# A deeper ring for expert weights, with gate and up weights signalled apart, in a mixture-of-experts inference step

## What is computed

```python
    eidx = gsel[:, None] * EXPERTS_PER_GROUP + top_i      # 2 of 32 experts for each token
    for e in range(N_EXPERTS):
        he = jax.nn.silu(hf @ w_gate[e]) * (hf @ w_up[e])
        out = out + combine[:, e:e + 1] * (he @ w_down[e])
    ...
    shf, scf = jnp.split((jax.nn.silu(c) @ w_ada_f + b_ada_f)[:, None, :], 2, axis=-1)
    return modulate(rms_norm(x, g_final), shf, scf)
```

## Time and profile before

| what | value |
|---|---|
| time, median of 3 runs | 886.25 us (883.65 to 887.63) |
| time of the profiled execution | 883.69 us |
| its span, first to last instruction | 881.9 us |
| mean granted TensorE clock | 0.952 of full |
| TensorE busy with matmuls | 794.0 us (90%) |
| VectorE busy | 526.8 us (60%) |
| ScalarE busy | 226.2 us (26%) |
| bytes moved by DMA | 203.57 MB, 231 GB/s over the span |

### The profile page before, as it was taken

How to read it: one execution, slowest core, us unless ns; L and a number is a source line. 1 busy time by engine, 2 the same in 40 slices (tenths; PEclk the granted TensorE clock), 3 DMA queues, 4 the chain that set the end, 5 groups by cost and what they waited for, 6 DMA issues and landing times. The chain is left out here.

```text
span 881.9 us, 12815 instructions
## 1 busy us (share of the span) xinstructions
PE 794.0 (90%) x5326; PEld 622.1 (71%) x5330; DVE 526.8 (60%) x779; ACT 226.2 (26%) x322; POOL 64.5 (7%) x113
## 2 busy tenths in 40 slices
PE   3799999989999999999999998179999997988876
PEld 1499997546889999999999687156666564544532
DVE  1768999999758799956554774813233223132146
ACT  4353233010423233267123232012111101010003
POOL 1100000000000000000000000012222222111110
PEclk9899999999999999999999999569999999897899
DMA  9935433797753123232444515969999999899925
GB/s 339 338 90 152 150 131 101 265 327 247 244 179 84 56 72 96 72 94 75 131 123 147 197 54 220 399 211 399 360 373 415 417 394 411 332 420 408 379 95 236
DMA packets 96302, 203.57 MB, mean 231 GB/s; under 512 B 9725, under 2 KB 68453, under 8 KB 79856
## 3 DMA queue, kind: packets, MB, share of 16 engines
q1 hardware_dynamic: 81760, 160.28, 50.4%
q10 hardware_dynamic: 8960, 33.36, 9.5%
q0 software_dynamic: 5520, 9.06, 2.8%
HBM read 198.84 MB, written 14.84 MB: 242 GB/s over the span
## 5 line engine op out<-in xcount | busy, mean ns | idle before, releaser
L1515 DVE SCALAR_TENSOR_TENSOR arena<-arena,VT 128x574 f32<-128x574 f32 x240 | 177.1, 808 | 0.1
L964 PE MATMUL PS<-arena 128*64 128x256 f32 (+1 forms) x1024 | 147.3, 409 | 24.8 <-issue 20.5
L964 PEld LDWEIGHTS PS<-arena 128*64 128x64 f32 (+1 forms) x1024 | 105.4, 156 | 58.9 <-issue 34.2
L680 PE MATMUL PS<-gH,wHA 128*128 128x272 f32 x608 | 126.8, 290 | 0.8 <-ACT arena L1148 0.8
L680 PE MATMUL PS<-gH,wLA 128*128 128x272 f32 x608 | 126.5, 289 | 0.0
L680 PE MATMUL PS<-gL,wHA 128*128 128x272 f32 x608 | 126.3, 289 | 0.0
L680 PEld LDWEIGHTS PS<-gH,wHA 128*128 128x128 f32 x608 | 94.7, 188 | 7.3 <-ACT arena L1148 4.4
L680 PEld LDWEIGHTS PS<-gH,wLA 128*128 128x128 f32 x608 | 95.8, 188 | 0.0
L680 PEld LDWEIGHTS PS<-gL,wHA 128*128 128x128 f32 x608 | 95.2, 189 | 0.0
L1823 DVE TENSOR_TENSOR arena<-PS,arena 128x256 f32<-128x256 f32 x19 | 8.1, 424 | 134.2 <-ACT arena L1266 134.2
L984 PE MATMUL PS<-arena 128*64 128x512 f32 (+1 forms) x256 | 69.1, 597 | 1.4 <-DVE arena L1827 1.4
(11 more groups left out here) (313 smaller groups left out, 1137.6 us busy)
## 6 DMA issues: line engine op xcount, KB each, us to landing
arena<-w_gate SPq DMA_DIRECT2D x31, 1024.0 KB, 10.9
arena<-w_up SPq DMA_DIRECT2D x31, 1024.0 KB, 17.8
arena<-w_down ACTq DMA_DIRECT2D x27, 1024.0 KB, 10.7
arena<-w_ada SPq DMA_DIRECT2D x24, 1024.0 KB, 6.7
arena<-w_in SPq DMA_DIRECT2D x40, 512.0 KB, 4.2
arena<-w_ada_f SPq DMA_DIRECT2D x8, 1024.0 KB, 5.0
arena<-x_prompt SPq DMA_DIRECT2D x8, 512.0 KB, 7.4
arena<-w_in SPq DMA_DIRECT2D x4, 1024.0 KB, 6.3
```

The costliest lines, as they stand in the source:

```text
L680: last = pe.matmul(PS[:, bank + h, 0:H], w[:, k, :], part[:, k, h * H:(h + 1) * H], start=(k == 0 and n == 0), stop=(k == KT - 1 and n == 2))
L964: last = pe.matmul(PS[h * rows:(h + 1) * rows, 2, n * DE:(n + 1) * DE], hG[:, b, k * SLOTS + h * rows:k * SLOTS + (h + 1) * rows], buf[r][ ...
L1515: dve.scalar_tensor_tensor(out=total, in0=src, scalar=tap, in1=total, op0=ALU.mult, op1=ALU.add).then_inc(conv_step, 1)
```

## The change

- The ring has five places for all loads: load n goes to place `n % 5`, the load before it in the place is n - 5.
- Gate and up loads have semaphores of their own (`gate_full`, `up_full`; the latter are taken over from earlier stages). `gate_up` waits for the tile's gate loads, multiplies, raises `gate_done`, then waits for its up loads, multiplies, raises `gu_done`.
- SyncE loads a gate array when `gate_done`, and an up array when `gu_done`, has reached the last use of the place. The expert's number is read ahead of both waits.
- The down loads of loads 30 and 31 are issued in tile 18 (elsewhere still in the tile after the last use of the place), behind a new wait of ScalarE for the up half of load 31.
- The final vectors are loaded after the down loads of 30 and 31 have landed and the up product of tile 18 is done (place 4 now holds load 29 until then).
- Four semaphores that only count begun steps become one.

```diff
-        gu_full = [sem(f"gu_full{r}") for r in range(5)]
+        gate_full = [sem(f"gate_full{r}") for r in range(5)]
+
+        up_full = ada1_in[TT:KT] + [ws_in, cache_in]
+        gate_done = sem("gate_done")
...
         def place_of(n):
-            return n if n < NSTATIC else (n - 1) % 4
+            return n % NSTATIC
 
         def before_it(n):
-            return n - 5 if n < NSTATIC + 4 else n - 4
+            return n - NSTATIC
 
         def uses(n):
-            return 1 if n < NSTATIC else (n - 1) // 4 + 1
+            return n // NSTATIC + 1
...
             for n in range(NSTATIC, LOADS):
+                e = owner_of(unit_of(n))
+                sp.wait_ge(gate_done, last_use[before_it(n)])
+                load_gate(place_of(n), e)
                 sp.wait_ge(gu_done, last_use[before_it(n)])
-                load_owned(unit_of(n), place_of(n))
-
+                load_up(place_of(n), e)
+
+            for n in in_tile[ALWAYS]:
+                sp.wait_ge(wd_full[place_of(n)], 16 * uses(n))
+            sp.wait_ge(gu_done, last_use[LOADS - 3])
             sp.dma_start(gfb, a["g_final"].rearrange("(o n) -> o n", o=1).to_broadcast([P, D])).then_inc(fin_in, 16)
...
-                slots = weights(i, t, gu_full, 32)
                 pe.wait_ge(hg_ready, cnt(i, t, 2))
-                rows = SLOTS // len(slots)
-                for n, buf in enumerate((WG, WU)):
+                for n, (buf, full_of, done) in enumerate(((WG, gate_full, gate_done), (WU, up_full, gu_done))):
+                    slots = weights(i, t, full_of, 16, 16 * n)
+                    rows = SLOTS // len(slots)
                     for k in range(KT):
                         for h, r in enumerate(slots):
                             last = pe.matmul(PS[h * rows:(h + 1) * rows, 2, n * DE:(n + 1) * DE],
...
-                last.then_inc(gu_done, 1)
+                    last.then_inc(done, 1)
...
                     for n in range(NSTATIC, LOADS):
-                        if last_use[before_it(n)] == t - 1:
+                        if t == (ALWAYS - 1 if n in in_tile[ALWAYS] else last_use[before_it(n)] + 1):
+                            if n == in_tile[ALWAYS][0]:
+                                act.wait_ge(up_full[place_of(LOADS - 1)], 16 * uses(LOADS - 1) + 16)
                             load_d(unit_of(n), place_of(n))
```

More of the change, by code:

```diff
@@ L262, in build @@
         mod_stored = [sem("mod_stored0"), sem("mod_stored1")]
-        loads_begun, turns_begun, gathers_begun, scatters_begun = (sem(n) for n in ("loads_begun", "turns_begun", "gathers_begun", "scatters_begun"))
+        begun = sem("begun")
         ada1_in = [sem(f"ada1_in{k}") for k in range(KT)]
@@ L937, in turn_rows @@
                 pe.wait_ge(gathered[b], cnt(i, t, 8, 8 * (1 - b)))
-                pe.sem_inc(turns_begun)
+                pe.sem_inc(begun)
                 if t >= 2:
                     pe.wait_ge(hg_ready, cnt(i, t, 2, -2))
-                    pe.sem_inc(turns_begun)
+                    pe.sem_inc(begun)
                 for k in range(KT):
@@ L944, in turn_rows, with weights @@
                 last.then_inc(t_ps, 1)
-            def weights(i, t, full_of, per):
+            def weights(i, t, full_of, per, earlier=0):
                 if t <= ALWAYS:
                     for n in in_tile[t]:
-                        pe.wait_ge(full_of[place_of(n)], per * uses(n))
+                        pe.wait_ge(full_of[place_of(n)], per * uses(n) + earlier)
                     return [place_of(n) for n in in_tile[t]]
                 for r, more in later(t):
-                    pe.wait_ge(full_of[r], cnt(i, t, per // 2, per // 2 * more))
+                    pe.wait_ge(full_of[r], cnt(i, t, per // 2, per // 2 * more + earlier))
                 return [r for r, more in later(t)]
             def gate_up(i, t, b):
-                slots = weights(i, t, gu_full, 32)
                 pe.wait_ge(hg_ready, cnt(i, t, 2))
-                rows = SLOTS // len(slots)
-                for n, buf in enumerate((WG, WU)):
+                for n, (buf, full_of, done) in enumerate(((WG, gate_full, gate_done), (WU, up_full, gu_done))):
+                    slots = weights(i, t, full_of, 16, 16 * n)
+                    rows = SLOTS // len(slots)
                     for k in range(KT):
```

29 lines of the change are left out of this document (16 added, 13 removed).

## The result

The change makes the kernel faster, by less than half of what was forecast. The median goes from 886.53 us (20 runs) to 880.35 us (20 runs, 876.52 to 884.76); the ratio is 0.9933 with a 95% interval of 0.992 to 0.9947, thus about 6 us, or 0.7%. The forecast was 873.4 with a range of 868 to 881.5.

A forecast was written before the change was run, and what follows sets the result against it. The kernel was taken to wait for weights, DMA being by turns full and held by the four-place ring. -8.5 -0.5 -4.5 +0.3 +0.3 = -12.9 us took the median from 886.25 to 873.4 us, range 868 to 881.5.

The forecast's parts named there:

- E: End of kernel: final vectors issued after the last down loads land make VectorE wait; cost 0.3 us, upper end 3.
- A: Weight ring: five places close the DMA holes in the experts' stage; gain 8.5 us, bounds 4.2 and 12.
- B: Last tiles: deferring down loads 30 and 31 gains 0.5 us; undeferred with five places they would take 5 us.
- U: Last tile: the moment up load 31 lands, 828.74 us in the profile before; expected at about 820 after the change.
- D: Last tile: the last down product may wait for its deferred loads; cost 0.3 us, range 0 to 6.5.
- so DMA needn't stand: Step of A: three experts' gate and up loads under way (15 us) outlast a tile's product, at most 10.08 us.
- one hole whose cause the issue times prove: DMA hole from 750 to 770 us, laid to SyncE issuing 24's gate load only at 761.59; worth 4.2 us.
- C: Last tile: the gate half runs while the up load is in flight; gain 4.5 us, range 2.6 to 6.5.
- rivals 1 and 4: First: ring gains little, 881, chance 0.09; fourth: gate half doesn't run ahead, 878, chance 0.10 shared with a middling A.
- little comes of the ring: DMA holes move instead of closing, as SyncE stands at two waits per load; 5 us less, 881, chance 0.09.
- The third one: End of kernel: deferred down loads and final vectors land late, costing 9.9 us; 3 us slower, 889, chance 0.06.
- DMA share of 0.97 or more until the last up load: Sign that the forecast is right: this share in every 20 us from 630 us on in the experts' stage.

The follow-up runs named there:

- e1: Kernel after, with ScalarE issuing the final vectors right behind down load 31, without waiting for its landing: 875.59 us, ratio 0.9883.
- e2: Kernel before (four places, its due times), with only gate and up loads split onto semaphores of their own: 881.87 us, ratio 0.994.
- e3: Kernel after, but gate and up not apart: products wait for both halves, places refill after the up product: 884.01 us, ratio 0.9973.
- e13: Kernel before, with each expert's rows laced over a half and the two halves levelled: 878.64 us, ratio 0.9914.
- e6: Kernel after without deferring down loads 30 and 31; final vectors wait only for tile 18's product: 880.14 us, ratio 0.9939.
- e14: e6 (five places, split, nothing deferred) with rows laced and halves levelled: 871.80 us, ratio 0.9842.
- e11: Kernel after, with each expert's rows laced over a half and the two halves levelled: 874.24 us, ratio 0.9862.
- e8: Kernel after, with each unit's rows turned round by twice the unit's number: 880.44 us, ratio 0.9933.
- e16: Kernel after, with down loads and final vectors in SyncE's queue in order of use, rows laced and halves levelled: 868.78 us, ratio 0.9809.
- e5: Kernel after without the expert stage's gathers and scatters, one even 0.46 MB ScalarE store a tile instead: 869.61 us (one run).

## Why the prediction was wrong in size

Two steps failed. The larger is E, the final vectors, 5.4 us; the other is A with B, which came 3 us short.

**E, final vectors (+0.3, up to 3): wrong, the step that cost most.** 5.67 us in the trace, 4.8 by e1, which takes it away. The working let the vectors follow "the down loads' landing, U + 9.2", which was the short end of D, while D's own cost of 0.3 puts that landing at U + 11.1 (10.8 + 0.3): two terms that share one moment had two values for it. With U + 11.1, the forecast's own 2.4 and 6.0 us give U + 19.5, against a weighing that ends at U + 16.1: about 3 us of cost and not 0.3. The rest is the time of the loads. From U + 10.6 SyncE issued five in 2.5 us. The last, one of the two of 128 KB, took 8.8 us, and the nearest row, 6.0, was of the second of two; behind one another the second to the fifth landed at 840.0, 841.5, 842.2 and 843.9. That is U + 21.2, 5.6 us behind the weighing's end at U + 15.6.

**A, five places (-8.5): its holes closed, but it was too large.** Measured are only sums: with B it had 9.0 at U and brought 5.8 by S (e2 to the kernel after), or 4.8 where gate and up were not apart (before to e3). If B is worth the 1 us at most that the forecast gave it with four places, A is about 4 to 6 us, an estimate from these runs, near the lower of its bounds of 4.2 and 12. The step that failed is "so DMA needn't stand", with the missing share of a mean taken for time that U would gain. The holes closed (1.02 and 1.01), the engines that were ahead ran further ahead, and in place of the holes the share was 0.55 for the last 17.7 us ahead of U. e2 shows it at its plainest: the split alone filled half of the early hole and most of the later one, and brought 0.9 us at U. With the rows dealt evenly kernels of four and five places both gain, and their distance does not grow to 8.5 (3.7 us with the deferring, 1.4 without). The "one hole whose cause the issue times prove" was proved only in part. Load 24 was issued late, at 761.59, but load 23 landed at 764.40, so its slowest engine was still at work on it: the share of 0.79 was a mean of engines that were done and engines that weren't. In e13, with four places and the rows dealt evenly, this hole is gone, while the early one (0.78) stays and was the ring's own.

**B, deferred down loads (-0.5, and 5 us if not deferred): the 5 us right.** e6 against the kernel after: 5.6 us at U. With the rows dealt evenly it is less, 2.3 us (e14's 232.9 to e11's 230.6). The 0.5 with four places was not tried.

**C, gate and up apart (-4.5, 2.6 to 6.5): right.** -5.35 in the trace, -5.3 by e2 (0.9 of that at U). The gate array landed 2.5 us ahead of U, the least that was foreseen, but the product ran at 7.13 us and not at tile 19's slow pace.

**D, the last down loads late (+0.3, 0 to 6.5): right**, 0.57. Down 31 landed at U + 10.5, near the U + 10.8 of the forecast, while the product ended 0.8 us earlier behind U than forecast.

In sum, against the forecast: U 3 us short of its 9 (of that 0.63 is a later start), E 5.4 us worse, D 0.3 worse, C 0.85 better. That makes 7.7 us, the whole distance between the profiled execution's 878.52 and the forecast's 870.8. The median of 880.35 lies inside the range of 868 to 881.5 only because its high end was drawn for rivals 1 and 4, neither of which is what happened; that is luck. Of the rivals, the first (881, "little comes of the ring") is nearest to what came, but its reason, two waits per load in SyncE's queue, isn't what the runs show. The third one's mechanism, deferred loads that make the vectors late, was there at half its price. Two of the signs to look for failed: the DMA share of 0.97 or more until the last up load (0.55 over the last 17.7 us), and VectorE "at most 2 us behind the weighing", which was 5.61 us.

The 358 GB/s of the Trainium skill ("DMA: Bandwidth & Descriptors", Specifications) were no limit here either: 413 to 421 GB/s over 20 to 206 us in several of these runs.

What stays open is how A and B divide, as four places with the deferring were not run. Open too is e11's spread of 14 to 16 us where rows explain 5.4 (and e8's 24.6 against 13.1). In e16, with one hardware queue beside the gathers, it is 5 to 7; in e5, with two hardware queues and no gathers, 2 to 4.5. Both queues together with indirect transfers seem to add to it, but no run shows how. It was also not tried whether gathers of only the rows that are there help.

## What to carry to other kernels

A DMA share below 1 is a mean over 16 engines; before you count a hole as room, look when the load that is under way lands, for a load is as late as its slowest engine. Where several loads share a semaphore, the order of its increments doesn't tell which load landed when. Gathers and scatters with empty rows put their bytes on whichever engines own the filled rows; spread the filled ones over all the engines' groups of four, and over both halves of 64. Whatever is moved behind "the last weights have landed" must be costed from that landing with the durations of a queue of such loads, and all terms must use the same moment.

## What was not expected of the hardware

- The sixteen engines drift apart over tens of microseconds: in the kernel after 26.3 us lie between the first and the last share of one 1 MB load, while the mean share from 750 to 770 us is 1.01.
- An empty row of an indirect transfer still is a packet of 4 bytes, 0.007 to 0.009 us, against 0.16 us for 4 KB and 0.31 us for 8 KB. So the rows that are there weigh far more than the empty ones, and they weigh on the engine of their place.
- A kernel's late loads can be evened out without moving a byte less: a few changed constants and a laced comparison gave 4.6 to 8.3 us in six pairs of runs (e11 to e16 against the same kernels without them), as much as the whole change under study.
